# Full 128x128 turns in the block merges of a delta-rule layer, and split panels for the query, key and value products of a latent attention

## The reference

```python
A = jnp.where(strict, jnp.einsum('bhncd,bhnsd->bhncs', kb, k) * decay, 0.0)
L = A + jnp.eye(CHUNK, dtype=A.dtype)
rhs = jnp.concatenate([v * beta[..., None], kb * jnp.exp(G)[..., None]], axis=-1)
sol = lax.linalg.triangular_solve(L, rhs, left_side=True, lower=True, unit_diagonal=True)
```

```python
q = (rms_norm_2(c_q, q_norm_g) @ w_uq).reshape(b_, l_, MLA_HEADS, QK_NOPE + QK_ROPE)
kv = (rms_norm_2(c_kv, kv_norm_g) @ w_ukv).reshape(b_, l_, MLA_HEADS, QK_NOPE + V_DIM)
k_nope, v = jnp.split(kv, [QK_NOPE], axis=-1)
...
s = jnp.einsum('bqhd,bkhd->bhqk', qb, k).astype(jnp.float32)
```

## Time and profile before

| | us |
|---|---|
| median of 3 runs | 1274.04 |
| profiled execution, device time | 1273.12 |
| profiled execution, span | 1271.2 |
| TensorE busy in the span | 1221.3 (96%) |
| VectorE (DVE) busy | 701.7 (55%) |
| ScalarE (ACT) busy | 492.0 (39%) |
| GpSimd (POOL) busy | 107.0 (8%) |

### The profile page before, as it was taken

One profiled execution on the slowest core, in us unless ns is written; L12 is line 12 of the kernel. 1 busy time (PEld: TensorE's weight loads), 2 busy tenths in 40 slices (PEclk: granted clock), 3 DMA queues, 4 the chain that ended last, 5 costly groups with the idle time before them and its releaser, 6 DMA issues.

```text
span 1271.2 us, 20461 instructions
## 1 busy us (share of the span) xinstructions
PE 1221.3 (96%) x8672; PEld 994.5 (78%) x8672; DVE 701.7 (55%) x1018; ACT 492.0 (39%) x774; POOL 107.0 (8%) x151
## 2 busy tenths in 40 slices
PE   2899999997999999999999999999999999999998
PEld 2577788787878888888888889798767678888886
DVE  4699878654468544323333457758456546334344
ACT  4543543665246323112222344223446663232232
POOL 4000004621011000000000110000012320000000
PEclk9899999999999999999999999999999999999999
DMA  9666621000222535233322343333231115433311
GB/s 311 219 209 184 219 66 36 3 3 31 74 67 71 163 105 160 81 111 104 100 87 63 86 146 94 100 92 76 41 79 46 34 47 134 115 87 87 114 40 67
DMA packets 150955, 125.62 MB, mean 99 GB/s; under 512 B 16985, under 2 KB 134514, under 8 KB 150737
## 3 DMA queue, kind: packets, MB, share of 16 engines
q1 hardware_dynamic: 147888, 119.88, 31.3%
q0 software_dynamic: 1232, 2.07, 0.5%
q10 hardware_dynamic: 1744, 2.36, 0.5%
HBM read 122.20 MB, written 2.10 MB: 98 GB/s over the span
## 4 chain that ended last, share of the span: by engine, by line
PE 91%; DVE 3%; DMA 2%; ACT 2%; issue 1%; POOL 0%; ACTq 0%; DVEq 0%; POOLq 0%
PE bank L583 56%; PE bank L676 5%; PE bank L825 5%; PE bank L1255 4%; PE bank L1226 4%; PE bank L1289 3%; PE bank L1143 2%; DMA arena<-in_meta_tokens_dram 1%; PE bank L988 1%; PE bank L1117 1%; PE bank L834 1%; PE bank L1176 1%; PE bank L1198 1%; PE bank L1156 1%; PE bank L797 1%
## 5 line engine op out<-in xcount | busy, mean ns | idle before, releaser
L583 PE MATMUL bank<-hsplit,whi 128*128 128x512 f32 (+1 forms) x1872 | 551.9, 379 | 0.7 <-DVE wlo L2005 0.7
L583 PEld LDWEIGHTS bank<-hsplit,whi 128*128 128x128 f32 x1872 | 341.2, 188 | 73.0 <-issue 8.0
L583 PE MATMUL bank<-hsplit,wlo 128*128 128x512 f32 (+1 forms) x936 | 352.3, 376 | 0.0
L2005 DVE TENSOR_TENSOR wlo<-ring,whi 128x2048 fp32r<-128x2048 f32 (+4 forms) x97 | 196.9, 2029 | 178.1 <-ACT whi L1485 177.8
L1485 ACT ACTIVATE whi<-ring 128x2048 fp32r<-128x2048 f32 (+4 forms) x97 | 165.4, 1705 | 129.3 <-DVE xT L2355 53.3
L583 PEld LDWEIGHTS bank<-hsplit,wlo 128*128 128x128 f32 x936 | 175.9, 188 | 33.1
L583 PE MATMUL bank<-a_split,whi 128*128 128x512 f32 x340 | 104.6, 389 | 0.0
L583 PEld LDWEIGHTS bank<-a_split,whi 128*128 128x128 f32 x340 | 63.8, 188 | 13.2
L583 PE MATMUL bank<-a_split,wlo 128*128 128x512 f32 x170 | 66.1, 389 | 0.0
L2034 DVE SCALAR_TENSOR_TENSOR post<-ring,small,post 128x512 f32<-128x512 f32 x77 | 57.9, 752 | 3.1 <-DMA ring<-in_w_ada_dram 0.4
L1426 POOL TENSOR_TENSOR acc<-acc,tb 128x512 f32<-128x512 f32 x12 | 17.7, 1478 | 426.2 <-ACT tb L1723 426.2
(11 more groups left out here) (443 smaller groups left out, 1726.2 us busy)
## 6 DMA issues: line engine op xcount, KB each, us to landing
ring<-in_w_ada_dram SPq DMA_DIRECT2D x24, 1024.0 KB, 5.2
ring<-in_w_in_dram SPq DMA_DIRECT2D x22, 1024.0 KB, 5.3
ring<-in_w_in_dram SPq DMA_DIRECT2D x34, 512.0 KB, 5.1
ring<-in_w_gate_dram SPq DMA_DIRECT2D x11, 1024.0 KB, 5.4
ring<-in_w_up_dram SPq DMA_DIRECT2D x11, 1024.0 KB, 5.2
ring<-in_w_down_dram SPq DMA_DIRECT2D x8, 768.0 KB, 4.9
ring<-in_w_down_dram SPq DMA_DIRECT2D x8, 640.0 KB, 4.5
ring<-in_w_out_dram SPq DMA_DIRECT2D x4, 1024.0 KB, 5.3
```

What stands on the lines that cost most here:

```text
L583: last = mm(o[0:m, 0:n], w[:, k, c0:c0 + m], rhs(s, k), start=k + i == 0, stop=k == kn - 1 and i == 2)
L2005: split_lo = splitter(dve, None, lambda lo, src, hi: tt(lo, src, hi, ALU.subtract))
```

## The change

It has two parts.

In the block merges, `t` becomes four 128x128 transposes for each pair of heads (a transpose turns two chunks of both heads at once, and leaves chunk parity, not head, on the partition halves). `z` is written by `heads_to_chunks` so that its rows lie by chunk parity too, and `c` by `chunks_to_heads` back to rows by head. The number of their 64x64 matmuls stays. A bank now holds one head or one chunk parity of two pairs of heads, so that the copies read 512 columns in another pattern and the subtractions on DVE come in quarters of 256 columns: 8 for each merge where there were 4 of 512. The split of one panel by DVE, which stood behind the first merge, stands behind the second.

In the latent attention, `uq` and `ukv` become split panels, and stand ahead of `gl00` in the list, not behind `gl01`. The query input is split while it is scaled (one more instruction on ACT for each half; on DVE the scaling becomes the rest), the key and value input after its norm. The key norm goes ahead of all queries on DVE. TensorE's waits for the last copies are spread over the loop, and the first gate quarter goes ahead of the first scores.

```diff
         t2_all, ta_all = (G1.take(NJ * T).rearrange("p (j t) -> p j t", j=NJ) for _ in range(2))
+        z_of_head = t1_all.rearrange("p j (b h c) -> p h j b c", b=NB, h=2)
+        bank_by_pair = lambda t: t.rearrange("p (j b c) -> p j b c", j=2, b=NB)
...
+        panel("uq", 2, 1024, [...])
+        panel("ukv", 1, 1024, [(0, slice(8 * s, 8 * s + 8), ukv_heads[:, s]) for s in range(2)])
         for m in range(KD):
             for h in range(2):
                 panel(f"gl{m}{h}", KD, 256, ...)
-            if m == 0:
-                panel("uq", 2, 1024, [...], split=False)
-                panel("ukv", 1, 1024, [...], split=False)
...
-            def crossed_products(name, j, left, right):
-                ...
+            all_quarters = ((0, 0), (1, 1), (0, 1), (1, 0))
+            def heads_to_chunks(name, j, left, right):
+                o = [open_tile(pe, name, j, h) for h in range(2)]
+                for i, b in product_order:
+                    for h, q in all_quarters:
+                        r, n, c = both_heads[h], 2 * b + q, (4 * i + b) * CH
+                        last = mm(o[h][both_heads[q], c:c + CH], left[j + i][r, n, :], right[j + i][r, n, :], start=True, stop=True)
+                        if (i, b) == product_order[-1] and (h, q) in all_quarters[2:]:
+                            last.then_inc(*fill(name, j, h))
+            def chunks_to_heads(name, j, left, right):
+                ...
+            product_order = [(i, b) for i in range(2) for b in range(NB)]
...
             for size, block, stage in ((16, a32, "a32"), (32, gA, "a64")):
                 for j in (0, 2):
                     for i in (j, j + 1):
-                        pe.wait_ge(*copied(before, i))
-                    crossed_products(f"t{size}", j, inv[j:j + 2], [lambda n: eye] * 2)
+                        if size == 16:
+                            pe.wait_ge(*copied("p3", i))
+                        elif i == j:
+                            pe.wait_ge(*copied("c32", j, 0))
+                            pe.wait_ge(*copied("c32", j, 1))
+                        o = open_tile(pe, f"t{size}", i)
+                        for b in range(NB):
+                            last = tr(o[:, b * P:(b + 1) * P], inv_flat[i][:, b * P:(b + 1) * P], ident)
+                        last.then_inc(*fill(f"t{size}", i))
...
-                    crossed_products(f"z{size}", j, block[j:j + 2], ...)
+                    heads_to_chunks(f"z{size}", j, block, inv)
...
-                    crossed_products(f"c{2 * size}", j, gW[j:j + 2], ...)
+                    chunks_to_heads(f"c{2 * size}", j, gW, gE)
...
+            three = ((0, 0), (0, 1), (1, 0))
+            pe.wait_ge(*done("w_lo", "uq"))
...
                 for k in range(2):
-                    last = mm(o[:, :], W("uq")[:, k, h * P:(h + 1) * P], cq[:, k, :], start=k == 0, stop=k == 1)
+                    for w, s in three:
+                        last = mm(o[:, :], uq[w][:, k, h * P:(h + 1) * P], cq_split[s][:, k, :], start=k + w + s == 0,
+                                  stop=k + w == 2)
...
             def ml_scores(u):
...
                     pe.wait_ge(*copied("q", h))
+                    pe.wait_ge(*copied("krsum", 0))
+                    pe.wait_ge(*copied("k", h // 2, 0))
+                elif u == 8:
+                    pe.wait_ge(*copied("krsum", 1))
+                    pe.wait_ge(*copied("k", 3, 1))
...
-            for half in range(2):
-                pe.wait_ge(*copied("krsum", half))
-                pe.wait_ge(*copied("k", 3, half))
-            pe.wait_ge(*copied("v", 3))
-            pe.wait_ge(*copied("v", 4))
...
+            mix_quarter(0)
             for u in range(len(MLU)):
                 ml_scores(u)
...
-                for x in range(4)[2 * u:2 * u + 2] if u < 2 else (u + 2,):
+                for x in ((1,), (2, 3))[u] if u < 2 else (u + 2,):
...
+            act.wait_ge(*done("ckvn"))
+            hi_part("ckv", (), ckv_split[:, 0, :], ckv)
...
-                for j in range(NJ):
-                    dve.wait_ge(*copied(before, j))
-                    gather(f"c{2 * size}", j, ALU.subtract)
-                split_lo()
+                        for i in range(2):
+                            if size == 16:
+                                dve.wait_ge(*copied("p3", j + i))
+                            blocks = inv[j + i][:, q::2, :]
+                            tt(blocks, blocks, bank_by_pair(bank(f"c{2 * size}", j, q)[:, :])[:, i], ALU.subtract)\
+                                .then_inc(*(read(f"c{2 * size}", j, q) if i else signal("part")))
+            split_lo()
+            split_lo()
```

More of the change, by code:

```diff
@@ L826, in product @@
                 return last
-            def crossed_products(name, j, left, right):
[L830 to L837, removed]
+            all_quarters = ((0, 0), (1, 1), (0, 1), (1, 0))
[8 more added lines that the diff above has]
+            def chunks_to_heads(name, j, left, right):
+                o = [open_tile(pe, name, j, q) for q in range(2)]
+                for i, b in product_order:
+                    for q, h in all_quarters:
+                        r, n, c = both_heads[q], 2 * b + h, (4 * i + b) * CH
+                        last = mm(o[q][both_heads[h], c:c + CH], left[j + i][r, n, :], right[j + i][r, n, :], start=True, stop=True)
+                        if (i, b) == product_order[-1] and (q, h) in all_quarters[2:]:
+                            last.then_inc(*fill(name, j, q))
+            product_order = [(i, b) for i in range(2) for b in range(NB)]
             def tile_product(name, j, left, right):
@@ L1125, in _ @@
                     o = open_tile(pe, "k", pair, half)
-                    mm(o[:, 0:TM // 2], wkv[:, pair * P:(pair + 1) * P], ckv[:, half * (TM // 2):(half + 1) * (TM // 2)],
-                       start=True, stop=True).then_inc(*fill("k", pair, half))
+                    for w, s in three:
+                        last = mm(o[:, 0:TM // 2], wkv[w][:, pair * P:(pair + 1) * P],
+                                  ckv_split[:, s, half * (TM // 2):(half + 1) * (TM // 2)], start=w + s == 0, stop=w == 1)
+                    last.then_inc(*fill("k", pair, half))
             for b in range(5):
@@ L1131, in _ @@
                     pe.wait_ge(*done("ckvrep"))
-                mm(o[:, :], ckv[:, META + b * P:META + (b + 1) * P] if b < 4 else ckvrep, wkv[:, 512:1024],
-                   start=True, stop=True).then_inc(*fill("v", b))
+                for w, s in three:
+                    tokens = ckv_split[:, s, META + b * P:META + (b + 1) * P] if b < 4 else ckvrep[:, s, :]
+                    last = mm(o[:, :], tokens, wkv[w][:, 512:1024], start=w + s == 0, stop=w == 1)
+                last.then_inc(*fill("v", b))
             last_tile_of["ukv"] = ("v", 4)
@@ L1415, in _ @@
             for j in range(NJ):
-                pool.wait_ge(*filled("z32", j))
+                for h in range(2):
+                    pool.wait_ge(*filled("z32", j - j % 2, h))
                 pool.wait_ge(*done("eglast", j))
@@ L1688, in _ @@
                     move(f"t{size}", j + 1, gW[j + 1])
-                    move(f"z{size}", j, gE[j])
+                    act.wait_ge(*filled(f"z{size}", j, 0))
+                    A(z_of_head[:, 0, j:j + 2], bank_by_pair(bank(f"z{size}", j, 0)[:, :]), ACT.Copy).then_inc(*read(f"z{size}", j, 0))
                 split_hi()
@@ L1815, in _ @@
                 A(cqsq[:, k, :], cq[:, k, :], ACT.Square).then_inc(*signal("cqsq", k))
+                act.wait_ge(*done("pool", 1))
+                A(cq_split[0][:, k, :], cq[:, k, :], ACT.Copy, scale=V1[:, V1_ROWS["q_norm"] + k:V1_ROWS["q_norm"] + k + 1])\
+                    .then_inc(*signal("cq_hi", k))
             split_hi()
@@ L2554, in _ @@
                 tt(conf_sum[:, m, :], conf_sum[:, m, :], conf_stats_[:, 1, :], ALU.mult).then_inc(*signal("cnorm", m))
+            dve.wait_ge(*done("ckvsq"))
+            for half in range(2):
+                dve.wait_ge(*copied("kvsum", half))
+            link(v.reciprocal(krb, krb))
+            stt(out=ckv, in0=ckv, scalar=col("kv_norm"), in1=krb, op0=ALU.mult, op1=ALU.mult).then_inc(*signal("ckvn"))
+            split_lo()
+            lo_part("ckv", (), ckv_split[:, 1, :], ckv, ckv_split[:, 0, :])
+            dve.wait_ge(*done("ckv"))
+            for s in range(2):
+                v.tensor_copy(ckvrep[:, s, :].rearrange("p (h k) -> p h k", h=8),
+                              ckv_split[:, s, 0:META].unsqueeze(1).broadcast_to([P, 8, META])).then_inc(*signal("ckvrep"))
             for m in range(2):
```

80 lines of the change are left out of this document (42 added, 38 removed).

## The result

| | us | of its before |
|---|---|---|
| before, median | 1274.01 (1273.32 to 1275.78) | |
| after, median of 6 | 1262.7 (1261.71 to 1264.81) | 0.991, 95% interval 0.9898 to 0.9922 |
| predicted | 1263.7 (1259.3 to 1268.8) | |
| span of the profiled execution | 1271.2 before, 1259.9 after | |

The kernel is 0.9% faster, 11.3 us by the spans. The page of the changed kernel has the same engine at the bound, with less for it to do: 195 matmul records fewer, TensorE 3.4 us less busy (the merges give up 224 records, the split products of the attention add 29). So most of the 11.3 is time in which TensorE had stood still.

The account below looks back on a forecast made before the run. TensorE was taken as the bound, short of instructions in the merges. Gains of 6.0 (merges) and 4.3 us (attention), 10.3 off 1273.1, gave 1262.8; with 0.9 for the median, 1263.7 us, range 1259.3 to 1268.8.

Parts of the forecast that it names:

- The bound: Whole kernel: TensorE, busy 96% of the span; in the block merges, instruction supply, a packet of about 256 each 3.6 us.
- The merges: Block merges: 1536 instructions fall to 1088, 6 packets to 4.25; first solution at 300.7, not 306.74; gain 6.0 us.
- the drain: New turns in the merges: switching between 128x128 and 64x64 tiling costs TensorE 0.14 us, eight times, 1.1 us in all.
- DVE's copies for the merges: Block merges: DVE's work per merge grows from 4 x 0.68 to 8 x 0.41 us, yet TensorE is not held up.
- The attention: Start of latent attention: cheaper split products and one wait less, 4.85 us, minus 0.6 of new wait; gain 4.3 us.
- The wait for L2586: Ahead of the first attention scores: TensorE's wait for the mask product, 1.05 us, goes.
- The new wait at the rotary keys' banks: Fifth and sixth query: ACT's slow rotary-key copies free the banks late; 0.6 us of new wait.
- The value tiles: Latent attention: first value tile wants its bank at 927.2, gets it at 927.1; no wait, but little room.
- Rival D: Attention gains nothing: ACT's split of `gl00` holds up value tiles and first gate quarter, 2.6 us lost; 1266.3 us, 11%.
- B: Rival: no gap left in the merges, packets being fetched during longer stretches of turns; gain 8.8 + 4.3, 1260.9 us, 14%.
- C: Rival: the merges' gaps belong to the dense 64x64 products, not instruction supply; about 1270.3 us, 9%.
- E: Rival: the attention loop stops being TensorE's, ACT and DVE working in turn; 18.9 us more, 1282.6 us, 4%.

Follow-up runs that it names:

- the filler: The kernel before with one more fp32 matmul of 256 columns ahead of each of the twelve product calls of the merges; 1274.54 us, one run.
- mla_only: The kernel before with the latent attention's part of the change alone, merges as they were; 1269.78 us, 0.9958 of before.
- waits_only: The kernel before with only TensorE's waits spread over the first units and a gate quarter ahead of the first scores, products still fp32; 1273.37 us.
- krsum_early: The changed kernel with ACT's two copies of the rotary keys ahead of the last gate panel instead of behind it; 1260.95 us, 0.9903 of before.
- merges_only: The kernel before with the merges' part of the change alone, attention as before; 1266.66 us, 0.9937 of before.

## Why the prediction was right, step by step

**The bound.** Right. The pauses were instruction supply: in the kernel before the large ones stand 256 instructions apart, give or take one, they follow a shift of 160 instructions to the record, and added work goes into them. The Trainium skill ("Runtime: NRT & Kernel Launch", section "Instruction fetch mechanics") has the size of a packet as these runs show it, but calls the cost of crossing one mostly hidden; here it was 8.0 us of 21.8 in one stage, and the measurement decides.

**The merges, 6.0 forecast, 6.2 found** (5.8 by the stage's own length; the rest is a start 0.3 earlier). The solutions were to start at 300.7 and start at 300.57; the pauses were to begin at about 290.95 and 298.7 and begin at 291.02 and 298.69. Three sizes were off and made up for one another. A turn takes 1.02 us and not 1.15: of its time over 8 x 0.11, only 0.14 is left for both changes of shape, so I charged the drain twice. A `z` takes 1.09 and not 1.0. And the row of the pause says 1.15 where I had 1.6, but the cut call takes 0.4 longer and 0.1 stands ahead of it, 1.65 in all. 4 x (1.02 + 1.09 + 1.05) + 2 x 1.65 = 15.9; the forecast was 15.8. So the mechanism was right, and that the sum came within 0.2 us of it was luck: three executions of the same merges took 15.0, 15.4 and 15.9 us, by the length of two pauses, so their gain is 5.8 to 6.7.

**DVE's copies for the merges** hold nothing up in the changed kernel, as forecast: the four of 256 columns run 0.33 us apart, and TensorE's next turn comes behind the pause. That cover is the pause itself; where the pause moved away, with 160 more instructions, TensorE waited 0.35 and 0.58 us for them.

**The attention, 4.3 forecast, 4.2 found.** The query product is 0.69 us, not 0.709, a key tile 2.92 / 8 = 0.365 (0.366), a value tile 0.74 with the start behind a wait, 0.70 without: 3.9 us in place of 3.8. The wait for L2586 was worth 1.08 (1.05). The new wait at the rotary keys' banks is 0.7 and not 0.6, at the fifth and sixth query and with the cause given; what I had not counted is that the first pair behind a wait takes 0.12 us longer, twice. Then 0.1 at the first value tile.

**The value tiles.** I had the first one's bank free 0.1 us before it was asked for; it came late. The chain of the changed kernel has ACT's key copy (L1908) right ahead of it, queued behind the split of `gl00` (1.92 us), and it costs 0.1 to 0.2 us. The other four and the gate quarter find all they need. Rival D's mechanism exists, with less than a tenth of its price of 2.6 us; as a rival it falls.

**The other rivals.** B (no pause left): falls, two are left of over a microsecond; the row for it (three packets in 22 us without a gap) only said that slow packets are hidden. C falls by the filler and by the moved borders. E falls: TensorE is busy for 95.89 of 96.00 us of the loop.

**The sum.** 10.3 forecast, 11.3 found by the spans. 0.2 of the difference is the merges, less 0.1 in the attention; 0.4 lies between the merges and the attention and 0.5 behind it. The forecast had put both at nothing. The 0.4 comes from the solutions, whose packet borders the change moved too: the kernel before, `mla_only` and `waits_only` have a pause of 0.33 us there and take 18.86 us, the changed kernel and `krsum_early` have none and take 18.2. It is not sure to be gained: `merges_only`, with the same border as these two, has a pause of 0.28 at it. Of the 0.5, 0.3 goes with the attention's part: ACT's last idle time is 0.34 us in the five kernels without its split panels and 0.04 in the five that have them. Why is open, and so is the 0.2 in the loop. None of this was forecast, and it is small beside what else moves: the start of the merges lay between 284.6 and 286.6 us among kernels with the same instructions ahead of them.

## What to carry to other kernels

Where TensorE stands still in "issue" in the middle of a run of small matmuls, count instructions: if the pauses are a fixed number of records apart, the stage is short of instructions, and fewer and larger ones pay more than their own busy time, while added work may be free. When a wait or a pause is taken away, work out who asks next and how much earlier: here both remaining costs (the copies of the rotary keys, the copies of `c`) had been hidden by what went. Two kernels that differ by a microsecond or two are told apart by marks inside their traces, not by their medians. But set the second mark behind all that the stage can push its cost into, and look at more than one execution: one and the same stage took 15.0 to 15.9 us here, and a gain of 0.9 in it was gone by the next mark.

## What was not expected

160 instructions that do nothing, put ahead of everything, change what happens 283 us later. In the kernel before they took 0.55 us off the merges, and off the stretch to the output product as well (55.01 us in three kernels, 54.46 with them, one execution). They also made the merges start earlier, by 1.2 us in the changed kernel (283.41 for 284.64) and 1.5 in the one before (283.46 for 284.98); in both the last of POOL's products before the merges begins as much sooner (278.20 for 279.44, 278.24 for 279.77). Why that is so was not tried, and it stays open. The pause at one and the same border was 0.55 us in one kernel and 1.16 in another: where it falls can be worked out beforehand, how long it lasts only to about half a microsecond. And crossing a border costs more than the idle row shows, 0.4 us more in the records on its two sides.
